# mLSTM states between the gates' weight pieces, HGRN projection behind them, a fifth ring slot, GpSimd as issuer of stores and row transfers

## The reference, cut to what matters

```
aq, af, ai, ag, bu, bv, bo, big, bfg, ga, gb = split(x @ w_in)
o_a, s_new = hgrn2_scan(silu(aq), key_a, log_f, ai, s_hgrn)
o_a = rms_norm_heads(o_a, a_norm_g) * silu(ag)
y_a = o_a @ w_pa
h_b, c_new, n_new, m_new = mlstm_scan(q_b, k_b, bv, i_pre, log_fg, c, n, m)
h_b = sigmoid(bo) * layer_norm_heads(h_b, b_norm_g)
y_b = h_b @ w_pb
out = (sigmoid(ga) * y_a + sigmoid(gb) * y_b) @ w_o
```

## Time and profile before

| | us |
|---|---|
| runs | 2489.67, 2495.30, 2492.04 |
| median | 2492.04 |
| profiled execution, its own time | 2495.11 |
| span of its profile | 2493.3 |
| mean granted PE clock in it | 0.935 |

### The profile page before, as it was taken

How to read it: one execution, slowest core, us unless ns; L and a number is a source line. 1 busy time by engine, 2 the same in 40 slices (tenths; PEclk the granted TensorE clock), 3 DMA queues, 4 the chain that set the end, 5 groups by cost and what they waited for, 6 DMA issues and landing times.

```text
span 2493.3 us, 31440 instructions
## 1 busy us (share of the span) xinstructions
PE 2257.2 (91%) x13220; PEld 1967.8 (79%) x13220; DVE 1593.3 (64%) x1806; ACT 1156.3 (46%) x1156; POOL 31.1 (1%) x51
## 2 busy tenths in 40 slices
PE   7898997799899998988996799789999999999996
PEld 6787764589799997877773699678888888888884
DVE  5745655655554435663746555478988978889893
ACT  4443331144243335353321243266766766767673
POOL 1000000000000000000000000000000000000000
PEclk9999987699999998999996799889999999999998
DMA  5223433734434432223614634469989999889980
GB/s 163 68 89 98 149 99 98 223 114 147 145 111 160 144 112 85 68 89 91 193 51 144 203 108 148 151 251 336 358 324 328 363 324 369 330 318 366 332 317 22
DMA packets 313739, 473.22 MB, mean 190 GB/s; under 512 B 15594, under 2 KB 189946, under 8 KB 313592
## 3 DMA queue, kind: packets, MB, share of 16 engines
q1 hardware_dynamic: 312476, 469.04, 54.8%
q10 hardware_dynamic: 1116, 2.10, 0.5%
HBM read 439.10 MB, written 29.92 MB: 188 GB/s over the span
## 4 chain that ended last, share of the span: by engine, by line
PE 74%; DVE 7%; ACT 5%; DMA 4%; ACTq 2%; issue 1%; SPq 0%; DVEq 0%
PE bank L528 11%; PE bank L530 11%; PE bank L529 11%; PE bank L534 9%; PE bank L535 9%; PE bank L536 9%; DMA out_c_sample<-weights 3%; PE bank L901 2%; ACT mixer_high L1141 2%; PE bank L877 2%; DVE mixer_rest L1627 1%; PE bank L623 1%; PE bank L713 1%; PE bank L740 1%; PE bank L851 1%
## 5 line engine op out<-in xcount | busy, mean ns | idle before, releaser
L1781 DVE TENSOR_TENSOR unit_rest<-weights,unit_high 128x2048 fp32r<-128x2048 f32 x198 | 452.1, 2290 | 87.0 <-ACT unit_high L1264 86.1
L1264 ACT ACTIVATE unit_high<-weights 128x2048 fp32r<-128x2048 f32 x198 | 379.3, 1919 | 160.3 <-PE bank L530 155.0
L1627 DVE TENSOR_TENSOR mixer_rest<-weights,mixer_high 128x2048 fp32r<-128x2048 f32 x96 | 219.5, 2288 | 226.6 <-ACT mixer_high L1141 226.5
L534 PE MATMUL bank<-tokens_in_high,mixer_high 128*128 128x320 f32 x896 | 286.4, 320 | 8.2 <-DVE tokens_in_rest L2263 6.4
L528 PE MATMUL bank<-unit_high,tokens_high 128*128 128x512 f32 (+1 forms) x768 | 291.2, 379 | 2.0 <-DVE tokens_rest L1787 2.0
L530 PE MATMUL bank<-unit_high,tokens_rest 128*128 128x512 f32 (+1 forms) x768 | 287.0, 374 | 0.0
L529 PE MATMUL bank<-unit_rest,tokens_high 128*128 128x512 f32 (+1 forms) x768 | 286.7, 373 | 0.0
L535 PE MATMUL bank<-tokens_in_rest,mixer_high 128*128 128x320 f32 x896 | 281.5, 314 | 0.0
L536 PE MATMUL bank<-tokens_in_high,mixer_rest 128*128 128x320 f32 x896 | 280.8, 313 | 0.0
L1141 ACT ACTIVATE mixer_high<-weights 128x2048 fp32r<-128x2048 f32 x96 | 182.9, 1906 | 133.7 <-PE bank L536 47.8
L534 PEld LDWEIGHTS bank<-tokens_in_high,mixer_high 128*128 128x128 f32 x896 | 174.0, 194 | 9.6 <-DVE tokens_in_rest L2263 6.9
(11 more groups left out here) (398 smaller groups left out, 4374.0 us busy)
## 6 DMA issues: line engine op xcount, KB each, us to landing
weights<-in_w_in SPq DMA_DIRECT2D x72, 1024.0 KB, 4.9
weights<-in_w_ex_gate SPq DMA_DIRECT2D x67, 1024.0 KB, 6.5
weights<-in_w_ex_up SPq DMA_DIRECT2D x66, 1024.0 KB, 6.3
weights<-in_w_ex_down SPq DMA_DIRECT2D x65, 1024.0 KB, 6.7
arena<-in_w_ex_down SPq DMA_DIRECT2D x23, 1024.0 KB, 6.5
arena<-in_w_ex_up SPq DMA_DIRECT2D x22, 1024.0 KB, 6.5
arena<-in_w_ex_gate SPq DMA_DIRECT2D x21, 1024.0 KB, 7.0
weights<-in_state_mlstm_c SPq DMA_DIRECT2D x16, 1024.0 KB, 6.2
```

What stands on the lines that cost most here:

```text
L534: nc.tensor.matmul(out, wh, xh, start=start, stop=False)
L1264: nc.scalar.activation(high[n % MOE_SPLIT], raw[n % MOE_RAW], ACT.Copy).then_inc(mo_high, 1)
L1627: nc.vector.tensor_tensor(wl, unit_at(l, *u)[0], wh, ALU.subtract).then_inc(*dv_s.done("unit rest", l, *u))
L1781: nc.vector.tensor_tensor(rest[n % MOE_SPLIT], raw[n % MOE_RAW], high[n % MOE_SPLIT], ALU.subtract)\
```

## The change

The order of PE's work between the heads' loop and pb is new, and all other engines follow it. The loads come in the order ga, bo, gb, pa, pb, wo, and a state stands behind each of the positions in `STATE_AFTER`:

ga00 (rms sums, normaliser rows) C0, ga01, C1, ga10, C2, ga11, C3, bo00, bo01, C4, bo10, C5, bo11, C6, gb00, C7, gb01 (inter_turned), gb10 (muB), gb11 (varB), pa00 (spread of varB), pa01, pa10, pa11, pb, wo.

Here ga01 is the second piece (part 1) of the first half of ga. In detail:

- The ring has a fifth slot from ga10 on, in the arena at `a_row` (`SLOTS`); its first load waits for the last head's spread. Some buffers move for that.
- ACT and DVE split a piece two positions ahead of its use in ga, bo and gb, three ahead in pa, pb and wo (`HIGHS_AFTER`). The first two, ga00 and ga01, are split in the heads' loop.
- The dC of a state is made at once after its interB, head by head, so that the eight matmuls of a state all use one group of 32 rows.
- DVE makes the HGRN norms of the heads `NORMS_AFTER[b]` after the update of state b, not two after each pair of states.
- The sigmoids of ga and bo are kept; pa is multiplied by the gate as it is evacuated.
- The variance of the mLSTM heads is summed to four rows (`head_rows`), inverted there by one reciprocal of 4 x 320, and spread by PE (`head_spread`). Norm, product with bo and the two halves are made per head between the pieces of pa. PE waits for all heads' rests before pb.
- GpSimd begins the 32 row transfers of a layer, the 4 stores of S and the 8 stores of C. SP only loads (and stores the small outputs); `store_heads` stands ahead of the load of ga10, not of C4.
- The first loads of the feed-forward part wait for the last content of their slot: slot 0 for wo10, 1 for wo11, 2 for pb11, 3 for wo00, in this order on SP, the fifth and sixth for wo11.

The core of the diff:

```
+STATE_AFTER = [0, 1, 2, 3, 5, 6, 7, 8]
+NORMS_AFTER = [[0], [1, 2], [3], [4, 5], [6], [7], [], []]
...
-    last = [(n, i) for n in ("pa", "ga", "bo", "gb", "pb", "wo") for i in range(2)]
+    last = [(n, i, part) for n in ("ga", "bo", "gb", "pa", "pb", "wo") for i in range(2) for part in range(2)]
...
+SLOTS = [i % RING if i < MIXER.index(("ga", 0, 0)) else (i - MIXER.index(("ga", 0, 0))) % (RING + 1) for i in range(NMIXER)]
+LAST_IN = {slot: MIXER[i] for i, slot in enumerate(SLOTS)}
...
+def highs_after():
...
+        at = MIXER.index(SPLIT[w]) - (2 if SPLIT[w][0] in ("ga", "bo", "gb") else 3)
...
+        ring = ring + [view(a_row, UNIT)]
...
+                g = slice(32 * (b % 4), 32 * (b % 4) + DS)
+                for h in range(HB):
+                    out = claim(pe, "W", l, "dC", b, h)
                     for c in range(2):
+                        mm = nc.tensor.matmul(out[:, c * 256:(c + 1) * 256],
+                                              kB4[g, b // 4, h * 256 + c * P:h * 256 + (c + 1) * P],
+                                              vB4[g, b // 4, h * 256:(h + 1) * 256], start=True, stop=True)
...
+                for name, i, part in TAIL:
+                    if name == "C":
+                        sampled_mlstm(l, i)
+                        continue
...
+                for h in range(HB):
+                    pe.wait_ge(*dv_s.at("hB rest", l, h))
...
-                for b in range(DB):
-                    g = slice(32 * (b % 4), 32 * (b % 4) + DS)
-                    act.dma_start(kA4[g, b // 4, :], kTok[DS * b:DS * b + DS, 2, :]).then_inc(spread_rows["kA"], 16)
-                    act.dma_start(vA4[g, b // 4, :], vTok[DS * b:DS * b + DS, 2, :]).then_inc(spread_rows["vA"], 16)
...
+                    if h == 2 or h == 3:
+                        unit_high(l, FIRST_HALF + h - 2)
...
+            def spread(name, dst, rows_, l):
...
+                    pool.dma_start(dst[g, b // 4, :], rows_[DS * b:DS * b + DS, 2, :]).then_inc(spread_rows[name], 16)
...
+                pool.wait_ge(*ac_s.at("st", l, 1))
+                spread("kA", kA4, kTok, l)
+                spread("vA", vA4, vTok, l)
+                for u in range(DB // 2):
+                    pool.wait_ge(*dv_s.at("newS", l, 2 * u + 1))
+                    pool.dma_start(O["hgrn_sample"][l, 2 * u:2 * u + 2].rearrange("b h k v -> k b h v"),
...
+                for b in range(DB):
+                    pool.wait_ge(*dv_s.at("newC", l, b))
+                    pool.dma_start(O["c_sample"][l, b].rearrange("h (c k) v -> k h c v", c=2),
...
-                    if i >= RING and MIXER[i - RING][0] in ("S", "C"):
-                        store_states(l, *MIXER[i - RING][0:2])
                     mixer_load(l, i)
...
+                            sp.wait_ge(*pe_s.at("unit", l, *LAST_IN[u]))
```

More of the change, by code:

```diff
@@ L112, in mixer_units @@
             out += [("S", 2 * i + part, 0), ("bv", i, part)]
-    out += [("C", i, 0) for i in range(DB)]
-    return out + [(n, i, part) for n, i in last for part in range(2)]
+    for n, u in enumerate(last):
+        out.append(u)
+        if n in STATE_AFTER:
+            out.append(("C", STATE_AFTER.index(n), 0))
+    return out
 MIXER = mixer_units()
 NMIXER = len(MIXER)
+TAIL = MIXER[MIXER.index(("ga", 0, 0)):MIXER.index(("pb", 0, 0))]
 SPLIT = [u for u in MIXER if u[0] not in ("S", "C")]
@@ L342, in build @@
         sqB = view(a_u, KC, T)
-        rsB = view(a_x, HB, T)
-        boS = view(a_x + 2 * H, KC, T)
+        rsB = view(a_x, T, rows=HB)
+        boS = view(a_v, KC, T)
         gbS = view(a_x + 4 * H, KC, T)
@@ L499, in unit_at @@
         def unit_at(l, name, i, part=0):
-            n = l * NMIXER + MIXER.index((name, i, part))
-            return ring[n % RING], ring_full[n % RING], 16 * (n // RING + 1)
+            n = MIXER.index((name, i, part))
+            used = l * SLOTS.count(SLOTS[n]) + SLOTS[0:n].count(SLOTS[n])
+            return ring[SLOTS[n]], ring_full[SLOTS[n]], 16 * (used + 1)
         def split_at_home(l, name, i, part):
@@ L714, in head_sums, with head_rows, head_spread @@
                     mm.then_inc(*pe_s.done(name, l, h))
+            def head_rows(l):
+                pe.wait_ge(*ac_s.at("sqB", l))
+                out = claim(pe, "M", l, "varB")[0:HB, 0:T]
+                for c in range(KC):
+                    h = c // 2
+                    mm = nc.tensor.matmul(out, one_of[:, 3 - h:7 - h], sqB[:, c, :], start=c == 0, stop=c == KC - 1)
+                mm.then_inc(*pe_s.done("varB", l))
+            def head_spread(l):
+                pe.wait_ge(*dv_s.at("rsB", l))
+                for h in range(HB):
+                    out = claim(pe, "W", l, "rsB", h)
+                    nc.tensor.matmul(out[:, 0:T], sel[:, h, :], rsB, start=True, stop=True).then_inc(*pe_s.done("rsB", l, h))
             def gates(l):
@@ L2348, in mixer_load @@
             def mixer_load(l, i):
-                if i >= RING:
-                    name, j, part = MIXER[i - RING]
+                if SLOTS[i] in SLOTS[0:i]:
+                    name, j, part = MIXER[max(n for n in range(i) if SLOTS[n] == SLOTS[i])]
                     if name in ("S", "C"):
```

386 lines of the change are left out of this document (207 added, 179 removed).

## The result

| | before | after |
|---|---|---|
| median of the runs, us | 2493.46 | 2457.17 |
| all runs | 2489.67 to 2495.30 | 2456.84 to 2459.62 |
| profiled execution, its time / its span | 2495.11 / 2493.3 | 2456.84 / 2455.1 |
| mean granted PE clock | 0.935 | 0.951 |

The ratio of after to before is 0.9859, with a 95% interval from 0.9841 to 0.9876: 35 to 36 us faster. The forecast was 2440, 52 us faster, with a range of 2420 to 2480. The direction, the range and the mechanism held; a third of the forecast gain did not come.

A forecast was written before the change was run, and what follows sets the result against it. PE, busy 91%, was taken to bound the kernel, losing time where state stores and loads alternate. Per layer −27.5 (stretch) and −4.8 (row transfers), +3 (issuer), +2 (clock), with +2.3 dense once: 52.3 us off, 2440, range 2420 to 2480.

The forecast's parts named there:

- gates and S states, up to the heads' end: Row transfers for kA and vA leave ACT's queue, so PE's 4.79 us wait ahead of the gates goes: −4.8 per layer.
- wait c: At muB: DVE's rest of pa01 stands ahead of the subtraction of the mean, 4.5 us per layer.
- waits (a) to (d): PE's expected waits around states, at bo01, at muB and ahead of pb: together 18.2 us per layer.
- GpSimd as issuer: Stores begun by GpSimd start 1 us later than SP's and move some late pieces: +3 us per layer.
- The clock: PE works at the low clock for a while after three waits of 5 us or so: +2, bounds 0 and 8.
- wait d: Ahead of pb: PE waits for all heads' rests, queued behind the rest of pb10, 6.5 us per layer.
- the ring: In the states' stretch, store and next load fit behind PE's work: 20.1 us needed in 23.3.
- Wait b: At bo01: DVE's updates and norms stand ahead of the rest of its weights, 5.1 us per layer.
- lead of 3.2 us: Spare time for ga11's load into C0's slot, counted with a store of 8.5 us.
- Rivals 1 and 2: Stores landing 2 to 4.5 us later, 2458 to 2485, chance 0.26; stores of 13.5 us or more, 2500 to 2510, 0.11.
- Rival 3: DVE's new order of norms and rests makes waits as long as the old ones: 2485 to 2497, chance 0.03.
- rival 4: Better: dC overlaps after all (−13 per layer), or the later waits shrink: 2405 to 2420, chance 0.04.

The follow-up runs named there:

- run 1: Against the changed kernel, each dC matmul runs over all 128 rows of the k and v buffers instead of its sequence's 8: 2428.0 us, ratio 0.9752.
- run 4: Against the changed kernel, only another order of norms, mean subtraction and halves on DVE and ACT: 2423.8 us; with head rests between pa's last evacuations, 2423.5.
- the last one: Against the kernel with 64-row dC on two row halves in turn (2398.7), ACT begins splitting the next piece one sigmoid earlier: 2379.8 us.

## Why the prediction was right, and what of it was not

The prediction's sum against the traces of before and after, us per layer (two figures are layer 0 and layer 1):

| term | forecast | measured |
|---|---|---|
| gates and S states, up to the heads' end | −4.8 | −7.8, −8.4 |
| 16 pieces | 112.6 | 129.4 |
| eight states | 36.8 | 38.1 |
| rms stretch | 6.6 | 7.2 |
| inter_turned, muB, varB and its spread | 11.9 | 13.8 (muB 6.3 instead of 4.3, at the low clock behind wait c) |
| waits (a) to (d) | 2.1, 5.1, 4.5, 6.5 | 0, 2.8, 3.2, 6.9 |
| stretch as a whole | −27.5 | −11.7, −15.4 |
| GpSimd as issuer | +3 | 0 (no wait on a load) |
| clock, apart from that | +2 | in the pieces and in muB above, and +2.1 in pb |
| dense loads | +2.3 | about +2 (wait 6.5 instead of 4.4), +1.0 net |

Together −16.3 in layer 0 and −21.9 in layer 1: PE's first dense matmul at 672.8 instead of 689.2, and the span 38.2 us shorter.

**The step that was mis-sized is "The clock"**: +2 us per layer, bounds 0 and 8, where the pieces took 16.8, muB's sums 2.0 and pb 2.1 more, 20.9 in all. It read the low clock of the earlier trace rows as the result of PE's waits and gave it to the three waits that were left. The rows of before can't part the two causes: in that stretch PE is idle for 28 of 75.5 us, and all its dC matmuls lie on 8 rows. What the new kernel does behind a state shows that PE need not be idle for it. It worked without a gap, and the clock fell behind dC's 3.7 us on 8 rows of 128; run 1 takes this apart from all else, and gives 29 us for it. Waits do their part as well: behind wait c and wait d muB's sums and pb are slow too, and are not any more where run 4 takes these waits away or shortens them. (The Trainium skill, "TensorE: Matmul & The Clock Gate", Part 1, explains the low level by how busy PE has been and warns of idle gaps; here the trace differs, since busy time was the same 4.72 us of 4.72 in both runs, and the measurement decides.)

**Luck in the number.** Three terms came out better than forecast and hid part of the clock: the waits (12.9 instead of 18.2), the gates and S states (7.8 and 8.4 instead of 4.8) and GpSimd as issuer (0 instead of 3), together some 23 us in both layers. Without them the time would have been 2480, at the very end of the range and with another cause than the rival's that stands there.

**The mechanism held.** The order removed the alternation of the earlier trace rows; the ring kept up; waits b, c and d stand at the places where the walk put them, with 12.9 us instead of 16.1. Wait b came out shorter than 5.1 because bo00, ahead of it, was itself slow (8.7 us): with the clock up (run 1) it is 4.3.

**The bounds of the store were far too careful.** The lead of 3.2 us was computed with 8.5 us, which was a shared transfer; landing in 5.1, the lead is 6.6, and even SP's stores and even four slots leave PE without a wait. Rivals 1 and 2 had 37 in 100 between them and were not near. What led there: no row of before showed a GpSimd transfer, and the landing of the earlier trace rows was taken for a property of the store without asking what else was under way; the first store, 4.4 us alone (section 5), would have told. Two small slips stand beside it: the packets of the stores were taken for the same (they are larger, 3.2 KB), and 32 pieces of 1.05 MB in 186 us are 180 GB/s, not 172. Neither changes the reading; the new stretch moved 174. (The Trainium skill, "SBUF — State Buffer", "SBUF: two separate sides", has GpSimd's descriptors held up by DVE's faster two-port modes; the forecast took it not to bite at the pace of this DVE, and the trace agrees: the store of C1 was begun at 422.31 us, 0.3 us behind the last update, and the stores landed in 5.1 beside a busy DVE.)

**ACT's issues were worth more than 4.8.** Taking back GpSimd's rows costs 20.5 us, 10.3 per layer: 7.2 before the heads' end, where the low clock behind the 4.8 us of waiting comes back too (gates 9.4 us instead of 7.19), and 3.2 at the square. The prediction had the second in its sum and the first without its clock.

Rival 3 was not near, though DVE's order did cost: 33 us by run 4. Of rival 4, dC did not overlap in the changed kernel (3.72 us for 16 records, the end that was taken), and did when it was given two groups of rows (2.00).

## What to carry to other kernels

- Where PE alternates between full matmuls and ones on few rows, look at the granted clock of the full ones behind. Widening the small matmuls to 64 or more rows, with masked operands that an idle engine makes, costs PE nothing and was worth 24 to 29 us of 2457.
- Before a landing time is put into a sum, ask what else was being moved in the same microseconds; divide the bytes of both by the time.
- Work that covers a preparation (here a state of 4.7 us over halves of 4.7) is a resource: whoever shortens it pays it back as a wait until the preparation begins earlier, as two runs here show (12.2 us per layer) and the last one mostly mends (3.4 left).
- Where the low clock falls on this piece or that one, two kernels differ by 1.5 us a piece. A difference of 5 us in 2450 is two such pieces per layer, and no finding by itself.

## What the runs showed of the hardware that was not expected

- PE's granted clock fell to the lower level behind 4.7 us of gapless work of which 3.7 were fp32 matmuls on 8 or 32 rows, behind seven of eight states in layer 0, and stayed at the upper one with the same matmuls on 64 or 128 rows (pieces 8.7 and 7.2 us).
- A 1 MB store begun by GpSimd took 0.9 us to issue and landed in 5.1; begun by SP in the same place 4.4, and 8.5 where a 1 MB load was begun 0.4 us ahead of it. GpSimd's queue moved 27.27 MB in packets of 3.2 KB on average.
- fp32 matmuls on rows 0 to 63 and 64 to 127 in turn, into two banks, overlap: 16 records in 2.00 us instead of 3.72.
